# Identity products queued on TensorE ahead of its waits, taken out of a two-block transformer kernel

## The reference

```python
def rms_norm(x, g):
    xf = x.astype(jnp.float32)
    y = xf * lax.rsqrt(jnp.mean(xf * xf, axis=-1, keepdims=True) + RMS_EPS)
    return (y * g.astype(jnp.float32)).astype(x.dtype)

def swiglu(h, w_gate, w_up, w_down):
    return (jax.nn.silu(h @ w_gate) * (h @ w_up)) @ w_down

def moe_swiglu(h, w_router, w_gate, w_up, w_down):
    logits = (h @ w_router).astype(jnp.float32)
    top_val, top_idx = lax.top_k(logits, TOP_K)
    top_w = jax.nn.softmax(top_val, axis=-1)
    gates = jnp.sum(jax.nn.one_hot(top_idx, N_EXPERTS, dtype=jnp.float32) * top_w[..., None], axis=-2)
    out = jnp.zeros_like(h)
    for e in range(N_EXPERTS):
        y = swiglu(h, w_gate[e], w_up[e], w_down[e])
        out = out + gates[..., e:e + 1].astype(h.dtype) * y
    return out
```

## Time and profile before

| | |
|---|---|
| median of 3 runs | 1796.07 us (1796.02 to 1798.53) |
| profiled execution, its own time | 1796.61 us |
| its span, first to last instruction | 1794.5 us |
| PE busy | 1760.4 us (98% of the span) |
| DVE busy | 1405.5 us (78%) |
| ACT busy | 1141.3 us (64%) |
| mean granted clock of PE | 0.998 |
| moved by DMA | 479.26 MB, mean 267 GB/s |

### The profile page before, as it was taken

One profiled execution on the slowest core, in us unless ns is written; L12 is line 12 of the kernel. 1 busy time (PEld: TensorE's weight loads), 2 busy tenths in 40 slices (PEclk: granted clock), 3 DMA queues, 4 the chain that ended last, 5 costly groups with the idle time before them and its releaser, 6 DMA issues.

```text
span 1794.5 us, 25476 instructions
## 1 busy us (share of the span) xinstructions
PE 1760.4 (98%) x9806; PEld 1521.9 (85%) x9806; DVE 1405.5 (78%) x1187; ACT 1141.3 (64%) x974; POOL 129.3 (7%) x137
## 2 busy tenths in 40 slices
PE   7999999999999999999999999999999999999998
PEld 6779999898888888888888888888888888789998
DVE  6566445656898989889889889898898879778665
ACT  6345444464677777777778777777777745746553
POOL 7000000000110000000000000000000008600000
PEclk9999999999999999999999999999999999999999
DMA  7445564542899999998999989999989843416561
GB/s 240 164 143 199 177 211 166 170 159 71 320 390 333 366 371 354 380 370 321 384 367 362 377 320 377 366 357 382 373 321 380 311 136 121 139 56 225 169 210 48
DMA packets 244356, 479.26 MB, mean 267 GB/s; under 512 B 11759, under 2 KB 80137, under 8 KB 244249
## 3 DMA queue, kind: packets, MB, share of 16 engines
q1 hardware_dynamic: 243385, 476.43, 74.3%
q10 hardware_dynamic: 864, 1.31, 0.2%
HBM read 476.66 MB, written 1.05 MB: 266 GB/s over the span
## 4 chain that ended last, share of the span: by engine, by line
PE 90%; DVE 6%; ACT 1%; issue 1%; POOL 0%; DMA 0%; DVEq 0%; SPq 0%; ACTq 0%; POOLq 0%
PE bank L2113 27%; PE bank L2115 27%; PE bank L2114 27%; PE bank L2570 1%; DVE wl L449 1%; PE bank L2526 1%; DVE xT L1378 1%; PE bank L2163 1%; PE bank L2375 0%; PE bank L2092 0%; PE bank L2164 0%; PE bank L2376 0%; PE bank L2379 0%; PE bank L2170 0%; PE bank L2607 0%
## 5 line engine op out<-in xcount | busy, mean ns | idle before, releaser
L1625 DVE TENSOR_TENSOR wl<-raw,wh 128x2048 fp32r<-128x2048 f32 x224 | 514.6, 2304 | 89.4 <-ACT wh L1060 88.2
L1060 ACT ACTIVATE wh<-raw 128x2048 fp32r<-128x2048 f32 x224 | 429.6, 1919 | 131.5 <-PE bank L2115 131.5
L2113 PE MATMUL bank<-wh,xTh 128*128 128x512 f32 x1088 | 431.4, 397 | 3.5 <-DVE wl L449 2.8
L2115 PE MATMUL bank<-wh,xTl 128*128 128x512 f32 x1088 | 424.6, 390 | 0.0
L2114 PE MATMUL bank<-wl,xTh 128*128 128x512 f32 x1088 | 423.8, 390 | 0.0
L449 DVE TENSOR_TENSOR wl<-raw,wh 128x2048 fp32r<-128x2048 f32 x112 | 254.8, 2292 | 64.5 <-ACT wh L442 62.6
L2113 PE MATMUL bank<-xTh,wh 128*128 128x256 f32 x944 | 268.0, 284 | 0.0
L2115 PE MATMUL bank<-xTh,wl 128*128 128x256 f32 x944 | 267.1, 283 | 0.0
L2114 PE MATMUL bank<-xTl,wh 128*128 128x256 f32 x944 | 267.1, 283 | 0.0
L1625 DVE TENSOR_TENSOR wl<-arena,wh 128x2048 fp32r<-128x2048 f32 x112 | 255.4, 2286 | 0.1
L1060 ACT ACTIVATE wh<-arena 128x2048 fp32r<-128x2048 f32 x112 | 215.2, 1922 | 50.7 <-PE bank L2115 50.7
(11 more groups left out here) (417 smaller groups left out, 1930.2 us busy)
## 6 DMA issues: line engine op xcount, KB each, us to landing
raw<-in_moe_w_up SPq DMA_DIRECT2D x112, 1024.0 KB, 7.5
arena<-in_moe_w_gate SPq DMA_DIRECT2D x96, 1024.0 KB, 7.4
raw<-in_moe_w_down SPq DMA_DIRECT2D x96, 1024.0 KB, 7.1
raw<-in_w_up SPq DMA_DIRECT2D x22, 1024.0 KB, 5.2
raw<-in_moe_w_gate SPq DMA_DIRECT2D x16, 1024.0 KB, 7.2
arena<-in_moe_w_down SPq DMA_DIRECT2D x16, 1024.0 KB, 7.0
raw<-in_gla_w_in SPq DMA_DIRECT2D x12, 1024.0 KB, 7.2
raw<-in_w_in SPq DMA_DIRECT2D x12, 1024.0 KB, 6.0
```

What stands on the lines that cost most here:

```text
L1060: V.activation(wh[:, s, :], src, ACT.Copy).then_inc(sg("hi_moe"), 1)
L1625: V.tensor_tensor(wl[:, s, :], moe_raw(c)[0], wh[:, s, :].bitcast(F32), ALU.subtract).then_inc(lo_moe, 1)
L2113: T.matmul(o, xh, yh, start=first, stop=False)
L2115: return T.matmul(o, xl, yh, start=False, stop=last)
```

## The change

The helper keep and its eleven calls go; everything else stays as it is, and in its order. Later lines move up, so L2092 becomes L2086, L2486 becomes L2478 and L2515 becomes L2502.

```diff
-            def keep(label, n):
-
-                ps = take(label)
-                for _ in range(n):
-                    T.matmul(ps[:, 0:P], ident[:, :], ident[:, :], start=True, stop=True)
-
...
-            keep(("n2", 0, 0), 4)
             norm("n2", order(False)[0:2])
-            keep(("n2", 1, 0), 4)
             tm_first(("sv", 0), "n2", 0, lambda: norm("n2", order(False)[2:4]))
...
             norm("n3", order(False)[0:2])
-            keep("pos", 4)
             logits(0)
-            keep("pos", 5)
             norm("n3", order(False)[2:4])
-            keep("pos", 2)
             done(logits(1), "lg")
-            keep("pos", 10)
             pe.wait_ge(sg("rt_sel"), 1)
...
-            keep("lg", 5)
...
-            keep(("n4", 0, 0), 12)
             norm("n4", order(False)[0:2])
-            keep(("n4", 1, 0), 4)
             pe.wait_ge(sg("ws_in"), 32)
...
-                    if hd == AH - 2:
-                        keep(("pT", hd), 5)
                     fox_transposes(hd)
...
-            keep(("yy", 0, 0), 4)
             transposes("yy", lambda t, half: pe.wait_ge(sg("o_a"), 1), order(True)[0:2])
```

## The result

The changed kernel is slower: a median of 1804.9 us (1802.71 to 1808.26, 6 runs) against 1796.09 us (6 runs) of before, a ratio of 1.0047 with a 95% interval from 1.0034 to 1.0061. Run again beside other kernels it had 1803.96 us against 1796.31, a ratio of 1.0040 (1.0027 to 1.0053). So taking the products out costs 7.7 to 8.8 us. The prediction said 1801.1 us, between 1794.9 and 1806.

What follows compares the result with a forecast made beforehand. PE was taken to bound the kernel, busy 1760.4 of 1794.5 us. Terms 1.6 (n2) - 1.2 (direct gains) + 3.7 (n3) + 0.9 (n4) = +5.0 us on 1796.07 gave 1801.1 us, range 1794.9 to 1806.

Steps and rivals of the forecast that it cites:

- the likeliest case: More clock drops at n2, n3 and n4: +3 to +9 us, own range 1799 to 1805, chance 0.55.
- The products cost nothing where they precede a wait: At n2, n4, fox head 6 and yy, removing the products gains 0 directly; at yy at most 0.4 us.
- n3, direct gain of 1.2 us: At n3, second tile's transposes start 0.89 us sooner and the gather 0.34 us sooner, together -1.2 us.
- n2, +1.6: At n2, a clock drop over the dense 512-column work behind the transposes costs 1.6 us, bounds 0 and 1.6.
- n3, +2.5 net: At n3, a drop behind logits(1) slows rank, count products and gather: +3.7 us, less the 1.2 gain.
- n4, +0.9: At n4, the clock may fall ahead of the transposes too, besides before's own drop: +0.9 us, bounds 0 and 2.5.
- yy and fox, 0: At yy and fox head 6, no added loss, as before drops at yy already; at most +1.6 us each.
- only long gaps count: Rival: n2 and n4 drop after long idle gaps, n3 does not; +1.3 us, 1797.4 us, chance 0.22.
- the products do nothing for the clock: Rival: remaining work holds the clock as well, drops stay where they were; -1.2 us, 1794.9 us, chance 0.10.
- Faster: Rival: the clock falls and recovers inside empty stretches of n4 and yy; -4.4 us, 1791.7 us, chance 0.05.
- Low through whole stages: Rival: clock low throughout n3 (+5.6), n2, n4 (2.5 each), yy and fox; +12.6 us, 1808.7 us, chance 0.08.
- The base: The kernel before, taken at 1796.07 us with two half-clock drops, in windows from 1441.10 and 1574.20.

Runs made afterwards that it cites:

- e6: The kernel before with 40 more identity products where PE still sat idle; 1792.75 us against 1796.31, ratio 0.9976.
- e5: The kernel before without the two groups of five products at n3 that seemed to hold PE up; 1801.12 us, ratio 1.0021.
- e7: e6 with the two groups that hold PE up at n3 cut from 5 to 1 and 5 to 3; 1793.17 us, ratio 0.9978.
- e11: e7 unchanged, profiled a second time; its slip within the experts against the first profile of before was 0.0 us.
- e12: e7 unchanged, profiled a third time; its slip within the experts against the first profile of before was 1.5 us.
- e2: The kernel before without the 8 products of n2 alone; 1798.65 us, ratio 1.0019.
- e1: The kernel before without the 26 products of n3 alone; 1800.81 us against 1796.39, ratio 1.0026.
- e3: The kernel before without the 16 products of n4 alone; 1800.26 us, ratio 1.0024.
- e4: The kernel before without the 5 products ahead of fox head 6 and the 4 ahead of yy; 1799.05 us, ratio 1.0010.
- e8: The changed kernel, unchanged, run and profiled again beside other kernels; 1803.96 us against 1796.31, ratio 1.0040.

## Why the prediction was right, point by point

The mechanism and the sign were as predicted, and n2, n3 and n4 as its places; the sum of +5.0 us was too small, against 7.7 and 8.8 measured. By the means of the profiles 6.5 us are lost at the places themselves, and the slip within the experts, which the prediction did not have, adds up to 1.5. The 1804.9 us lie inside the range of the likeliest case (1799 to 1805) by 0.1 us only.

- *The products cost nothing where they precede a wait* (n2, n4, fox, yy): right. The fill of e6 made no start later by more than 0.05 us.
- *n3, direct gain of 1.2 us*: the 0.89 for the transposes was right (0.9 in e5, e7, e11 and e12). The 0.34 for the gather was not: I gave the signal 0.05 us, which was right for the signal, but left out the waits that PE still had to go through behind it; together they take 0.36.
- *n2, +1.6*: 2.9 and 1.5 in the changed kernel's two profiles, 2.8 in e2, against a before that loses nothing there in its first profile and 1.6 in its second. On the mean 1.3, so the size was right, but by two errors against each other: a fall was not always as short as the one seen (6.7 us in two of three profiles), and before has falls there too.
- *n3, +2.5 net*: mis-sized. 3.8 and 3.1 measured, 3.0 in e1. Without the gain of 0.9 at the transposes the losses are 4.7, 3.9 and 3.9, against the 3.7 taken, and the gather's gain of 0.3 was not there to set against them. I had placed the fall behind logits(1), at the largest hole. It came before it in all three, at 444.2, 442.9 and 445.1 us. The reading "by share" failed: I compared 0.56 with the rows ahead of before's falls (0.40 and 0.50), but ahead of n3's falls PE worked for 4.60 (changed kernel) and 4.11 (e1) of 5.30 us, while the 3.11 of 5.30 from 316.80 on had kept the clock. The share of busy time did not tell where it falls. In e1 this work was almost all transposes and 8-column products; which of them fails to hold the clock was not tried. That the 8-column products double was a guess and right: 3.58 us for 1.92.
- *n4, +0.9*: mis-sized. 1.2 and 0.8 on a before that had its own drop, 1.6 in e3; but two of six profiles with these products in have no drop there, and against their mean it is 1.7.
- *yy and fox, 0*: as far as the profiles tell, about right, 0.2 on the mean. The distance grew by 0.5, 2.7 and 1.1 there, but by 0 to 3.0 with the products in as well. The ratio of e4 (1.0001 to 1.0019) says that it is more than nothing.
- *Rivals*: that only long gaps count fell with e1. Its n3 falls though no gap in the 5.3 us ahead is above 0.70 us, and none within it above 2.17. The section of the Trainium skill named with that rival ("TensorE: Matmul & The Clock Gate", "HAM oscillation — how this bites in real kernels") puts the fall down to an idle gap between bursts; this trace does not agree. (The 1.16 us given for the drop at 1574 hold for the last 3.2 us; 6 us before it stood a wait of 1.70.) That the products do nothing for the clock fell with e6. "Faster" never showed: none of the 11 runs of the changed kernel is below 1802. "Low through whole stages" came near in n3 (3.8 net where it had 4.4) and was too much for n2 and n4.
- *The base*: I took the drops of one profile for those of before. They vary; before's 56 executions spend 10.4 us at 0.50 on the mean, by the same measure its first profile 7.2.

## What to carry to other kernels

When PE is the bound and a chain of short steps on other engines makes it wait, look at the granted clock behind the wait, not at the wait: the idle time cost nothing here, the slow work around and behind it some 6 to 7 of the 8 us. Work without use, queued ahead of a wait and shorter than it, was free here and mostly kept the clock up; before it is trimmed or removed, the places where it holds PE up should be told from those where it fills, by what time the awaited signal came. And as the stretches at half clock come and go from one execution to the next, a single profile shows whether a place can fall, while how often it does takes the mean clock of many executions.

## What the runs showed of the hardware

- The gather of n3 starts 0.36 us behind the DVE instruction that frees its last bank (changed kernel, e1, e5, e7, e8, e11, e12). The signal is 0.04 us of it; the rest is PE's way through the wait instructions that stand behind the one held up, about 0.1 us apart. At the transposes of n2 the start came some 0.03 us behind the half of xn (about 317.86 to 317.89). Whether the gather starts sooner when the wait for that bank stands last was not tried.
- A stretch at 0.50 lasted 3.3 or 6.7 us at n2, and with the products out 13.5 to 16.9 in n3, 10.1 or 13.6 at n4 and up to 10.2 in the mixer. At n2 it was 6.7 us twice when it began 0.8 to 0.9 us ahead of the dense work, and 3.3 when it began 0.3 us ahead of it (e8) or behind its start (e1).
- The longest idle time of PE in the 5.3 us before the clock fell in n3 of e1 was 0.70 us, and PE was busy for 4.11 of these 5.30 us.
- The 8 transposes of 128 columns take 1.04 us at 1.00 and 1.95 at 0.50, the 16 products of 8 columns 1.92 and 3.58; both hold 128 columns of weights.
- In e4's profile the granted clock reads 0.95 from 18 to 1444 us, but the 512-column products are as long as in before (395 and 390 ns between 500 and 1400 us in both; columns: count, busy us, mean ns), so that figure says nothing of the speed; this profile is left out of the table above:

```profile
18.00:1444.00 1426.00, 1413.16 (x7372) 1207.70 (x7371) 1131.87 (x824) 939.77 (x726) 47.82 (x58) 0.95 0.82 298
```

```profile
L2113 PE MATMUL bank<-wh,xTh 128*128 128x512 f32 x828 | 327.4, 395 | 0.0
L2115 PE MATMUL bank<-wh,xTl 128*128 128x512 f32 x827 | 322.5, 390 | 0.0
```

- Between executions of one kernel PE's way through the experts differed by 0 or 1.5 us at a granted clock of 1.00.
